# Delta rule and spatial gate: layer-norm scaling on ACT, the inverse's diagonal halves by one DVE operation, the spatial bias from a table

## The reference, cut to what matters

```
u, v = split(gelu(h @ W_uv))                         # 512 features each
v    = (v - mean(v)) * rsqrt(var(v) + eps) * ln_g + ln_b
gate = einsum(ws[g], v per chunk of 128 tokens) + bs[g]     # 4 groups, ws is 128 x 128
y_a  = u * gate

# delta rule, per head, direction and chunk: A is strictly triangular (keys x keys, decayed)
T    = inv(I + A)
new values = T @ (beta * v) - T @ (beta * decay * k) @ state
```

## Time and profile before

| | us |
|---|---|
| median of 3 runs | 1693.4 (1692.94 to 1694.81) |
| the profiled execution | 1694.11 |
| its span, first to last instruction | 1692.0 |

### The profile page before, as it was taken

One profiled execution on the slowest core, in us unless ns is written; L12 is line 12 of the kernel. 1 busy time (PEld: TensorE's weight loads), 2 busy tenths in 40 slices (PEclk: granted clock), 3 DMA queues, 4 the chain that ended last, 5 costly groups with the idle time before them and its releaser, 6 DMA issues.

```text
span 1692.0 us, 30969 instructions
## 1 busy us (share of the span) xinstructions
PE 1572.8 (93%) x11422; PEld 1380.7 (82%) x11422; DVE 1141.4 (67%) x1913; ACT 786.4 (46%) x1416; POOL 115.2 (7%) x130
## 2 busy tenths in 40 slices
PE   5899978789999999999989999999999889999998
PEld 3687768688777777788778589999898668999997
DVE  5975755554499999967455558885566665477644
ACT  2554543132354444432255457775444445566532
POOL 2000032220200000001000010001000001010000
PEclk8999988899999999999989999999899999999999
DMA  8344420000245555555432034556444223255562
GB/s 355 120 177 156 150 70 2 1 3 1 100 148 178 187 182 187 185 177 170 137 134 88 25 100 162 184 187 212 161 163 147 89 75 99 101 184 186 178 194 90
DMA packets 62906, 230.50 MB, mean 136 GB/s; under 512 B 6816, under 2 KB 8096, under 8 KB 62304
## 3 DMA queue, kind: packets, MB, share of 16 engines
q1 hardware_dynamic: 61408, 223.37, 38.8%
q0 software_dynamic: 1120, 5.54, 1.0%
q10 hardware_dynamic: 288, 0.33, 0.1%
HBM read 228.17 MB, written 1.05 MB: 135 GB/s over the span
## 4 chain that ended last, share of the span: by engine, by line
PE 79%; DVE 11%; ACT 5%; issue 3%; POOL 1%; DMA 1%; DVEq 0%; ACTq 0%; POOLq 0%
PE proj L646 21%; PE proj L648 20%; PE proj L647 20%; DVE w_low L2068 2%; PE bank L698 1%; ACT w_high L1571 1%; PE bank L901 1%; PE bank L918 1%; PE bank L1198 1%; PE bank L921 1%; DVE conv_mid L2148 1%; DMA ident_sb<-ident 1%; PE bank L949 1%; PE proj L1102 1%; DVE mod_products L2199 1%
## 5 line engine op out<-in xcount | busy, mean ns | idle before, releaser
L646 PE MATMUL proj<-h_high,w_high 128*128 128x256 f32 (+1 forms) x1768 | 583.7, 330 | 22.7 <-DVE h_low L2101 14.3
L648 PE MATMUL proj<-h_high,w_low 128*128 128x256 f32 (+1 forms) x1768 | 570.4, 323 | 0.0
L647 PE MATMUL proj<-h_low,w_high 128*128 128x256 f32 (+1 forms) x1768 | 570.1, 322 | 0.0
L2068 DVE TENSOR_TENSOR w_low<-w_raw,w_high 128x1024 fp32r<-128x1024 f32 x322 | 393.1, 1224 | 190.1 <-ACT w_high L1571 188.7
L1571 ACT ACTIVATE w_high<-w_raw 128x1024 fp32r<-128x1024 f32 x322 | 338.2, 1054 | 244.0 <-PE proj L648 240.4
L646 PEld LDWEIGHTS proj<-h_high,w_high 128*128 128x128 f32 x1768 | 335.9, 190 | 65.5 <-issue 18.5
L648 PEld LDWEIGHTS proj<-h_high,w_low 128*128 128x128 f32 x1768 | 336.4, 190 | 27.5
L647 PEld LDWEIGHTS proj<-h_low,w_high 128*128 128x128 f32 x1768 | 335.9, 190 | 25.0
L646 PE MATMUL proj<-act_high,w_high 128*128 128x256 f32 (+1 forms) x608 | 190.4, 313 | 0.4 <-DVE w_low L2068 0.4
L648 PE MATMUL proj<-act_high,w_low 128*128 128x256 f32 (+1 forms) x608 | 189.6, 312 | 0.0
L647 PE MATMUL proj<-act_low,w_high 128*128 128x256 f32 (+1 forms) x608 | 188.9, 311 | 0.0
(11 more groups left out here) (406 smaller groups left out, 1920.5 us busy)
## 6 DMA issues: line engine op xcount, KB each, us to landing
w_raw<-w_stream SPq DMA_DIRECT2D x322, 512.0 KB, 3.3
a_ring<-a_stream SPq DMA_DIRECT2D x80, 512.0 KB, 3.2
a_first<-a_head SPq DMA_DIRECT2D x4, 1024.0 KB, 17.9
a_first<-a_stream SPq DMA_DIRECT2D x4, 1024.0 KB, 18.6
x<-x_in SPq DMA_DIRECT2D x1, 2048.0 KB, 10.5
late_tab<-late_tables POOLq DMA_DIRECT2D x1, 1408.0 KB, 6.6
cond_rows<-cond_rows SPq DMA_DIRECT2D x1, 1024.0 KB, 5.9
cond_rows<-cond_rows POOLq DMA_DIRECT2D x1, 1024.0 KB, 5.1
```

The costliest lines, as they stand in the source:

```text
L646: mm(out_, wh, xh, start=first, stop=False)
L647: mm(out_, wh, xl, start=False, stop=False)
L648: return mm(out_, wl, xh, start=False, stop=last)
L2068: v.tensor_tensor(wl(n), RAW[:, n % 4, :], wh(n), ALU.subtract).then_inc(w_low, 1)
```

## The change

Four things are altered:

1. Layer-norm scaling of st 0, steps 18 to 21: DVE's L2298, (x - mean) * r, is replaced by ACT's Identity with scale r and bias -mean * r. DVE computes -mean * r (128 x 4) at step 17 and raises `ln_r` a second time, for which ACT waits. DVE's gain product L2300 then waits for ACT (`ln_n`).
2. Level 5: DVE writes the result of steps 20 to 23 to `TH`, both halves in one operation. ACT copies the halves from `TH` to `TU` in its steps 22 to 25 (`lv_tc`), in both st, behind its `M1` copy. The last second product reads `TH` in place of `TU`. PE waits for `lv_tc` before L949.
3. Spatial bias: `BS` is a 128 x 512 table, loaded from the host's tiled copy. PE no longer makes the row product L841; its four group products start on their own. DVE adds product and table into the place of V (`sp_b`).
4. The multiplication by U goes to POOL, at its steps 8, 10, 12 and 14 of st 1 (`sp_y`); ACT waits for `sp_y` before it splits the result.

```diff
         "gdn_tables": gdn, "late_tables": late, "ident": np.eye(P, dtype=f),
         "ws_t": np.ascontiguousarray(a["a_ws"][0].transpose(2, 0, 1)),
-        "bs_row": a["a_bs"][0].reshape(1, 512),
+        "bs_row": np.tile(a["a_bs"][0].reshape(1, 512), (P, 1)),
         "ln_rows": np.tile(np.concatenate([a["a_ln_g"][0], a["a_ln_b"][0]]), (P, 1)),
...
         M1 = place("lev_m1", [P, 2, HEADS, 64])
         WS = place("ws_sb", [P, 4, P])
-        BS = place("bs_sb", [1, 512])
+        BS = place("bs_sb", [P, 512])
         decay_at = cursor[0]
...
                     pe.wait_ge(G["gb_e"], 16)
                     if t >= 2:
-                        pe.wait_ge(G["sp_y"], t - 1)
-                    mm(PL[t % 2][:], ONES[0:1, :], BS[:], start=True, stop=False)
+                        pe.wait_ge(G["sp_b"], t - 1)
                     for g in range(4):
                         o = PL[t % 2][:, g * P:(g + 1) * P]
-                        last = mm(o, UV[:, 4 + g, t * P:(t + 1) * P], WS[:, g, :], start=False, stop=(g == 3))
+                        last = mm(o, UV[:, 4 + g, t * P:(t + 1) * P], WS[:, g, :], start=True, stop=True)
                     last.then_inc(G["sp_s"], 1)
...
                 if k == 10:
-                    pe.wait_ge(G["sp_y"], 4)
+                    pe.wait_ge(G["sp_b"], 4)
                     out_sums(0)
...
                         x = last_half(q)
                         for h in range(HEADS):
-                            last = mm(out_u[first_half(q), h, :], M1[x, b, h, :], TU[x, q, h, x], start=True, stop=True)
+                            last = mm(out_u[first_half(q), h, :], M1[x, b, h, :], TH[x, q, h, :], start=True, stop=True)
                     last.then_inc(G["lv_x"], 1)
...
                 pe.wait_ge(G["lv_tu"], NSTEP * (st + 1))
+                pe.wait_ge(G["lv_tc"], 4 * (st + 1))
                 for q in range(4):
...
                     if st == 0 and k == 10:
                         pool.dma_start(BS[:], bs_row).then_inc(ws_in, 16)
+                    if st and k in (8, 10, 12, 14):
+
+                        t = k // 2 - 4
+                        x = slice(t * P, (t + 1) * P)
+                        pool.wait_ge(G["sp_b"], t + 1)
+                        nc.gpsimd.tensor_tensor(UV[:, 0:4, x], UV[:, 0:4, x], UV[:, 4:8, x], ALU.mult).then_inc(G["sp_y"], 1)
                     if st == 0 and 22 <= k < 26:
...
                     act.wait_ge(G["ln_sq"], 4)
                     f(SM[:, 58:62], SM[:, 58:62], ACT.Sqrt, scale=1.0 / 512, bias=col("eps")).then_inc(G["ln_std"], 1)
+                if 18 <= k < 22:
+                    t = k - 18
+                    x = UV[:, 4:8, t * P:(t + 1) * P]
+                    act.wait_ge(G["ln_r"], 2)
+                    f(x, x, ACT.Identity, scale=SM[:, 58 + t:59 + t], bias=SM[:, 54 + t:55 + t]).then_inc(G["ln_n"], 1)
...
                     x = slice(0, P) if k < NSTEP - 4 else last_half(k % 4)
                     f(M1[x, k % 2, :, :], BK[k % 2][x, 0:4 * 64].rearrange("p (h j) -> p h j", h=HEADS), ACT.Copy).then_inc(G["lv_m1"], 1)
+                    if 22 <= k < 26:
+
+                        q = k - 22
+                        act.wait_ge(G["lv_tu"], NSTEP * st + 21 + q)
+                        if st == 0 and q == 0:
+                            act.wait_ge(G["u_zero"], 1)
+                        for x in HALVES:
+                            last = f(TU[x, q, :, x], TH[x, q, :, :], ACT.Copy)
+                        last.then_inc(G["lv_tc"], 1)
                     values(st, k)
...
             for t in range(4):
+                act.wait_ge(G["sp_y"], t + 1)
                 f(HH[:, 0:4, t * P:(t + 1) * P], UV[:, 0:4, t * P:(t + 1) * P], ACT.Copy).then_inc(G["sp_hi"], 1)
...
                     v.reciprocal(SM[:, 58:62], SM[:, 58:62]).then_inc(G["ln_r"], 1)
                     dve.wait_ge(G["ln_r"], 1)
+                    v.tensor_tensor(SM[:, 54:58], SM[:, 54:58], SM[:, 58:62], ALU.mult).then_inc(G["ln_r"], 1)
                     dve.wait_ge(ws_in, 48)
...
                     t = k - 18
                     x = UV[:, 4:8, t * P:(t + 1) * P]
-                    v.tensor_scalar(x, x, SM[:, 54 + t:55 + t], SM[:, 58 + t:59 + t], ALU.add, ALU.mult).then_inc(G["ln_n"], 1)
                     dve.wait_ge(G["ln_n"], t + 1)
...
                 if 4 <= k < 8:
                     t = k - 4
-                    x = UV[:, 0:4, t * P:(t + 1) * P]
                     dve.wait_ge(G["sp_s"], t + 1)
-                    v.tensor_tensor(x, x, PL[t % 2][:].rearrange("p (a b) -> p a b", a=4), ALU.mult).then_inc(G["sp_y"], 1)
+                    v.tensor_tensor(UV[:, 4:8, t * P:(t + 1) * P], PL[t % 2][:].rearrange("p (a b) -> p a b", a=4),
+                                    BS[:].rearrange("p (a b) -> p a b", a=4), ALU.add).then_inc(G["sp_b"], 1)
...
                         if lev < NLEV - 1:
                             v.tensor_tensor(TT[:, q, :, :], TT[:, q, :, :], halves_of(2 + 2 * b), ALU.subtract)
-                        if lev < NLEV - 2:
                             last = v.tensor_tensor(TH[:, q, :, :], TH[:, q, :, :], new, ALU.subtract)
-                        elif lev < NLEV - 1:
+                        else:
                             if st == 0 and q == 0:
                                 dve.wait_ge(G["u_zero"], 1)
-                            for x in HALVES:
-                                last = v.tensor_tensor(TU[x, q, :, x], TH[x, q, :, :], new[x], ALU.subtract)
-                        else:
                             x = first_half(q)
```

4 lines of the change are left out of this document (2 added, 2 removed).

## The result

The changed kernel takes 1678.9 us (median of 5 runs, 1674.91 to 1686.6) against 1694.6 us of the kernel before beside it (1692.94 to 1694.81): ratio 0.992, 95% interval 0.990 to 0.993. Forecast were 1681.0, in a range of 1675.5 to 1688.5. The total was right. Two of its terms were not, and they nearly cancelled.

A forecast was written before the change was run, and what follows sets the result against it. The delta-rule chain was taken as bound by PE, by DVE in two places, and by clock falls. St 0 6.9, table 4.3 and halves in st 1 1.2 sum to 12.4 us off: forecast 1681.0 us, range 1675.5 to 1688.5.

The forecast's parts named there:

- The sign of being wrong: St 0: the prediction would be wrong if, among other signs, the granted clock fell about 275 us after all.
- rival A: End of st 0: the clock falls all the same, losing the 4.1 us; 8.3 off, 1685.1 us; chance 0.22.
- DVE relief in st 0: Steps 18 to 23: PE gets back 3.6 us of idle time, less 0.4 for slower L2300: 3.2 us.
- the halves' 1.7 us: Level 5, each st: one DVE operation replaces two halves, four times 0.42 us, so 1.7 us less on DVE.
- The two other small bets: St 0: M1(19) late makes SP(19) 0.6 us later, absorbed in waits; M1(26) about 0.4 us late, on the path.
- ACT's costs: Steps 18 to 25: Identity 0.72 us, half copies 0.38 each; with M1 1.1 to 1.14 a step, under 1.40.
- Rival C: ACT becomes the late engine, every M1 behind a transferred operation; no change, 1693.6 us; chance 0.08.
- Clock in st 0: 275 to 285.2 us: the clock holds once PE's waits go, giving 2.6 plus 1.5, together 4.1 us.
- Table, 4.3 us: St 1, steps 4 to 7: PE loses row products of 5.15 us; 3.15 count whole, the first as 1.15.
- Halves in st 1: Steps 20 to 24: three of four 0.42 us operations are on the chain; 1.2 us, bounds 0.4 and 1.7.
- rival B: End of st 1: the clock holds there too, 3.1 us more; 15.5 off, 1677.9 us; chance 0.13.
- Rival D: St 1: without L841 the clock stays low until the scan; 27.6 us slower, 1721 us; chance 0.04.

The follow-up runs named there:

- late additions: POOL's four layer-norm bias additions in st 0 moved two steps later: on the changed kernel 1680.2 us, 0.9919; on the kernel before 1693.3 us, 1.0015.
- layer norm alone: The kernel before with only the layer-norm scaling moved from DVE to ACT: 1692.5 us, ratio 1.0007.
- the displaced kernel: The changed kernel with ten 128x128 products that do no work on PE in step 7 of st 1: 1687.8 us, ratio 0.997.

## Why the prediction was right, and where it was not

**The sign of being wrong came.** The prediction said that it would be wrong if the clock fell about 275 after all. It fell at 275.3, and L949 of st 0 started at 277.65, not near 275. So the total was met with one mechanism missed, by clock gained in places that I had not counted. That is luck, and more of it lies in the median: the two profiled executions took 1686.6 and 1686.3 us, beside rival A's 1685.1.

**DVE relief in st 0, 3.2 us: right in kind, 2.5.** DVE was the late engine there; up to L925, at full clock in both kernels, the stretch went from 15.9 to 13.4 us. What was too low was the lengthening of L2300 beside POOL. It was put at 0.4, at most 1.6; the four gain products took 5.06 us, where three of 0.69 and one of 1.09 had stood, 1.9 more. That contention is what takes most of the halves' 1.7 us in st 0: 0.65 us up to L925 alone and 0.55 on top of the layer norm (14.0 to 13.4), with the gain products at 3.87 us without the halves and 5.06 with them. The late additions gave 1.35 back. The two other small bets held: M1 late at step 19 by 0.61 (0.6 said); PE waits for the late M1 in the last level, 0.6 (0.4 said).

**ACT's costs: low, without harm.** The Identity with two pointers took 0.81 us (0.72 said, from the square with one), a half copy 0.42 (0.38), the small product on DVE 0.38 (0.2). The Trainium skill, "ScalarE: Activation LUTs", Rules for kernel authors, prefers VectorE for such arithmetic; on the single instruction the trace agrees even more than I said, 0.81 against 0.55. Rival C did not come, since M1 with a transferred operation is 1.2 us in a step of 1.4. But the late additions on the kernel before show that about half of DVE's relief, 1.0 of 1.9 us, had nothing to do with ACT.

**Clock in st 0, 4.1 us: wrong, about 1.4.** This is the step that failed, and it was rival A. I reasoned that PE would work no less than at 364 to 368, where the clock had held, so it would hold. It worked more, 5.95 of 7.00, and the clock fell; with 5.65 at the same place it held in another kernel. A busy share read in one place is no forecast for another. What was left of the term is 0.4 us behind L949, where 2.6 stood in the sum, and ahead of it an estimate of 1.0 where 1.5 stood: L925 to L949 went from 5.0 to 4.6 us, although it now holds 0.6 of waits for M1. The size was about right for a clock that holds: the layer norm alone, with 1.00 all through, took 1.2 and 2.5 us less in these two stretches.

**Table, 4.3 us: right in mechanism, low by 1.6 (5.9).** Three row products in high clock gave 3.15, as said. The rest, 2.8 where I said 1.15 and 2.0 at most, is the first row product, 1.0 at full clock, and again the clock. Before, 8.4 us of st 1 lay in low clock (from L894 at 321.2 to the rise at 329.6), after it 4.5 (318.5 to 323.0), since that fall came earlier and lasted 6.8 us instead of 10.2; 3.9 us less of low clock are 1.9 us (an estimate, half of 3.9). The multiplications on POOL were covered as worked out.

**Halves in st 1, 1.2 us: low, 2.1.** From the keys to the end of the last fold of level 5 it went from 10.1 to 8.5 us, 1.5 less, between the 1.26 I took and the 1.7 of my upper bound. The other 0.5 lies between that fold and L949 and is the sum of two things that I had not priced: before, the fall at 377.4 came 2.9 us ahead of L949 (380.3), at half clock; in the changed kernel ACT's copies and the M1 behind them are on the chain there, from 366.6 to 367.9.

**The end of st 1, not in the sum: 1.8 us, rival B.** I spoke against it because the wait for DVE before SP(25) would stay. The rival's price was 3.1; the 1.8 is from L949 on, and the part ahead of L949 is in the 0.5 above. The clock held, but not because of anything in that stretch, as the displaced kernel shows.

**In sum** 2.9 (root to L949) + 0.4 (L949 to L978) + 5.9 + 2.1 + 1.8 = 13.1 us of the 13.6 between L894 and the next projection (the rest lies ahead of the root and behind the scan), against 12.4 said. Of them I had placed 4.1 on the clock in st 0; it gave about 1.4 there and about 4 in st 1. Rival D didn't strike either trace of the changed kernel. A long low stretch such as it feared is possible: one execution of the kernel before with late additions lost 10.5 us to one.

That the parts make 14 us together and 5 alone goes with the clock, by the mean clock of the runs and by the stretches; for the medians this is a relation and not a test. That the same work can be followed by a fall or by none is shown by the displaced kernel and by the untouched code; that it is the moment that decides is the reading that fits both. What the moment is measured against, and why all three parts together bring more of the run into the fortunate position in run after run, stays open.

The Trainium skill, "Advanced Engine Details and Errata", VectorE Performance Modes, says that GpSimd shares VectorE's second port and that it and VectorE's two-port instructions block each other. The trace agrees for operations with both inputs in SBUF (L2321, 1.78 us beside L1507 at 1.26), and for one of POOL's mask products (1.18 instead of 0.73), while another, beside the first gain product, stayed at 0.73. DVE's foldings, which read one input from PSUM, stayed at 0.41 beside POOL.

## What to carry to other kernels

Before moving work off a late engine, look at what runs beside it: here the group whose longest instance was twice its shortest (L2298, 0.55 to 1.12) was slowed by a neighbour, and putting the neighbour two steps later gave half of what moving the work gave. Where a stretch is compared, split it where the clock changes. A saving of a few microseconds in a kernel with such clock falls can be given back by what it displaces, so test it by parts, by pairs and by a plain displacement, and read the mean clock beside each median before you credit a part. And judge by medians: two profiled executions differed by half of what the medians did.

## What the runs showed of the hardware, unexpected

- The granted clock fell in one kernel and held in the other after the same work: 8.96 and 8.97 us of PE in 10 us at the end of st 1, 2.29 and 2.30 in 4 us near 1270. 2.2 us of busy PE put ahead of such a place cost some 9 us of the median, 6.8 of them seen in the trace.
- Once low, it stayed at half for 34 us in one execution (312.1 to 346.2), 26 us of them with PE busy without a gap.
- A product of two SBUF operands on DVE took 0.69 us alone, 1.04 to 1.12 beside POOL's mask product and up to 1.78 beside POOL's addition, whose own 1.26 us did not grow.
- ACT's Identity on 128x512 with both scale and bias from pointers took 0.81 us, against 0.72 for the square with one.
